# A split-precision encoder layer on one core: another order for the first token tiles of the value projection

## What is computed

```python
proj = x @ w_in
qa, ka, va, qb, kb, vb = jnp.split(proj, cuts, axis=-1)   # va: 128 columns, vb: 512
...
oa, _ = banded_attention(qa, ka, va, ...)     # windowed, with sinks and ALiBi
ob = dilated_attention(qb, kb, vb, ...)       # three dilations, merged
return jnp.concatenate([rms_norm(oa, norm_a), rms_norm(ob, norm_b)], -1) @ w_out
```

## Time and profile before

| | us |
|---|---|
| runs, median (lowest to highest) | 1284.3 (1279.02 to 1286.18) |
| the profiled execution | 1276.83 |
| its span, first to last instruction | 1275.0 |
| TensorE busy | 1212.4 (95%) |
| VectorE busy | 734.3 (58%) |
| ScalarE busy | 579.1 (45%) |
| GpSimd busy | 213.5 (17%) |
| mean granted TensorE clock | 0.977 |

### The profile page before, as it was taken

One profiled execution on the slowest core, in us unless ns is written; L12 is line 12 of the kernel. 1 busy time (PEld: TensorE's weight loads), 2 busy tenths in 40 slices (PEclk: granted clock), 3 DMA queues, 4 the chain that ended last, 5 costly groups with the idle time before them and its releaser, 6 DMA issues.

```text
span 1275.0 us, 22105 instructions
## 1 busy us (share of the span) xinstructions
PE 1212.4 (95%) x8045; PEld 1089.4 (85%) x8045; DVE 734.3 (58%) x1790; ACT 579.1 (45%) x1416; POOL 213.5 (17%) x276
## 2 busy tenths in 40 slices
PE   7999999999999999998899999998899999999993
PEld 6998788888888888887687888897799999999892
DVE  3232355665665556554667887548666556665478
ACT  3332244543554444434443343220366666666455
POOL 0120001200120021001111122000223323333222
PEclk9999999999999999999899999999899999999997
DMA  7697664365437453678535333442799999999783
GB/s 231 223 300 247 157 152 102 76 172 115 113 83 183 96 123 89 157 192 229 163 120 189 127 136 117 157 169 67 239 307 276 289 287 272 272 280 302 190 306 145
DMA packets 165106, 237.47 MB, mean 186 GB/s; under 512 B 41584, under 2 KB 111472, under 8 KB 164976
## 3 DMA queue, kind: packets, MB, share of 16 engines
q1 hardware_dynamic: 146096, 176.61, 46.0%
q0 software_dynamic: 11776, 41.95, 13.3%
q10 hardware_dynamic: 7152, 17.83, 4.3%
HBM read 147.44 MB, written 59.02 MB: 162 GB/s over the span
## 4 chain that ended last, share of the span: by engine, by line
PE 79%; issue 6%; DVE 4%; DMA 4%; SPq 2%; ACT 2%; POOL 1%; DVEq 1%; ACTq 0%; POOLq 0%
PE bank L843 18%; PE bank L845 17%; PE bank L844 17%; PE bank L944 9%; PE bank L837 5%; PE bank L931 5%; PE bank L922 4%; PE bank L923 2%; SPq L583 2%; PE bank L1066 2%; DMA Q<-stage_lo 1%; DMA KA<-stage_lo 1%; SPq L579 1%; DMA a_work<-in_x 1%; DMA d_work<-x_scratch,idc 1%
## 5 line engine op out<-in xcount | busy, mean ns | idle before, releaser
L1330 ACT ACTIVATE b_work<-b_work 128x256 f32<-128x256 f32 (+3 forms) x288 | 148.0, 514 | 244.9 <-DVE b_work L1680 244.8
L843 PE MATMUL bank<-xgT_hi,w_gu_hi 128*128 128x224 f32 (+1 forms) x704 | 197.6, 281 | 4.4 <-ACT d_work L1562 2.3
L844 PE MATMUL bank<-xgT_lo,w_gu_hi 128*128 128x224 f32 (+1 forms) x704 | 196.4, 279 | 0.0
L845 PE MATMUL bank<-xgT_hi,w_gu_lo 128*128 128x224 f32 (+1 forms) x704 | 196.3, 279 | 0.0
L1689 DVE COPY b_work<-bank 128x256 f32<-128x256 f32 (+2 forms) x256 | 112.7, 440 | 125.4 <-PE bank L931 124.6
L843 PEld LDWEIGHTS bank<-xgT_hi,w_gu_hi 128*128 128x128 f32 x704 | 136.7, 194 | 6.6 <-issue 3.1
L844 PEld LDWEIGHTS bank<-xgT_lo,w_gu_hi 128*128 128x128 f32 x704 | 136.7, 194 | 0.7
L845 PEld LDWEIGHTS bank<-xgT_hi,w_gu_lo 128*128 128x128 f32 x704 | 136.9, 194 | 0.0
L2196 POOL CAST Q<-Q 128x512 fp32r<-128x512 f32 x48 | 52.1, 1117 | 451.0 <-DVE w_k_lo L1636 236.5
L931 PE MATMUL bank<-keep,b_work 128*128 128x128 f32 x608 | 115.2, 275 | 6.2 <-ACT b_work L1330 6.2
L931 PEld LDWEIGHTS bank<-keep,b_work 128*128 128x128 f32 x608 | 80.5, 140 | 41.3 <-ACT b_work L1330 11.5
(11 more groups left out here) (214 smaller groups left out, 2844.8 us busy)
## 6 DMA issues: line engine op xcount, KB each, us to landing
raw_gu<-in_w_gate SPq DMA_DIRECT2D x32, 512.0 KB, 8.7
raw_gu<-in_w_up SPq DMA_DIRECT2D x32, 512.0 KB, 9.5
raw_d<-in_w_down SPq DMA_DIRECT2D x16, 1024.0 KB, 9.6
Q<-stage_hi SPq DMA_DIRECT2D x96, 128.0 KB, 2.4
Q<-stage_lo SPq DMA_DIRECT2D x96, 128.0 KB, 2.4
o_scratch<-b_work SPq DMA_DIRECT2D x36, 264.0 KB, 3.3
c_work<-o_scratch SPq DMA_DIRECT2D x12, 792.0 KB, 5.6
wo_scratch<-a_work POOLq DMA_DIRECT2D x16, 512.0 KB, 5.5
```

The lines of the kernel that those rows point to most:

```text
L843: nc.tensor.matmul(o, w_hi, x_hi, start=first, stop=False)
L844: nc.tensor.matmul(o, w_hi, x_lo, start=False, stop=False)
L845: return nc.tensor.matmul(o, w_lo, x_hi, start=False, stop=last)
L1330: nc.scalar.activation(prob[:, u % 2, 0:n], prob[:, u % 2, 0:n], ACT.Exp, scale=-1.0, bias=o[:, HD:HD + 1], accum_out=o[:, HD + 1:HD + 2])\
```

## The change

Seven edits, all in the first stage:

1. TensorE's queue begins with six 128x128 products of a tile of ones, into bank 7, which nothing reads. They wait only for VectorE's memset of the ones.
2. SyncE issues the identity ahead of x 0, and x 1 behind the first value slab's two loads.
3. For tiles 0 and 1 the hand-over of `xT` goes by halves of four pieces (one bank): new semaphores `xt_half`, `xs_half`, `xts_half`. Tile 1's banks are 2 and 3 as before. ScalarE and VectorE take half a tile and a weight slab by turns.
4. TensorE's loop over slabs starts a tile when its first half is there and asks for the second half at slab 4.
5. Tile 2 is transposed behind slab 5 of that loop, not after it. TensorE's wait for `v_ready` of tile 0, which ScalarE's order implied before, is now written out ahead of tile 2's products.
6. x 4 is no longer behind the first store of values, the three loads of gains stand ahead of it, and the other small loads behind x 5.
7. The eight steps of the output weights are each one tile earlier.

```diff
-WO_TILES = (3, 4, 5, 6, 7, 8, 9, 10)
+WO_TILES = (2, 3, 4, 5, 6, 7, 8, 9)
...
+            sp.dma_start(ident, const[:, 0:P]).then_inc(S["id_loaded"], 16)
             sp.dma_start(xin[:, 0, :], x_t[0]).then_inc(x_ld[0], 16)
-            sp.dma_start(ident, const[:, 0:P]).then_inc(S["id_loaded"], 16)
-            sp.dma_start(xin[:, 1, :], x_t[1]).then_inc(x_ld[1], 16)
             for k in range(KD):
+                if k == 1:
+                    sp.dma_start(xin[:, 1, :], x_t[1]).then_inc(x_ld[1], 16)
...
             load_w(KA0, KA0 + HD)
+            load_gains()
+            load_x(4)
             for t in range(4, TILES):
                 store_v(t - 4)
-                load_x(t)
-                if t == 4:
+                if t > 4:
+                    load_x(t)
+                if t == 5:
                     load_small()
...
+            pe.wait_ge(S["ones_ready"], 1)
+            for c in range(6):
+                nc.tensor.matmul(bank[7][:, 0:P], ones, ones, start=True, stop=True)
             pe.wait_ge(S["id_loaded"], 16)
+
+            def xt_first(t):
+                pe.wait_ge(x_ld[t], 16)
+                for c in range(KD):
+                    made = nc.tensor.transpose(bank[2 * t + c // 4][:, P * (c % 4):P * (c % 4) + P],
+                                               xin[:, t, P * c:P * c + P], ident)
+                    if c % 4 == 3:
+                        made.then_inc(S["xt_made" if c > 4 else "xt_half"], 1)
...
                 pe.wait_ge(S["xts_ready"], t + 1)
+                if t == 2:
+                    pe.wait_ge(S["v_ready"], 1)
...
-            xt(0)
-            xt(1)
-            pe.wait_ge(S["xts_ready"], 2)
+            xt_first(0)
+            xt_first(1)
             for k in range(KD):
                 pe.wait_ge(S["wv_made"], k + 1)
                 for t in range(2):
+                    if k == 0:
+                        pe.wait_ge(S["xts_half"], t + 1)
+                    if k == KD // 2:
+                        pe.wait_ge(S["xts_ready"], t + 1)
                     for c in range(2):
                         last = vpart(t, k, c)
                     if k == KD - 1:
                         last.then_inc(S["v_made"], 1)
-            xt(2)
+                if k == 5:
+                    xt(2)
...
-            xt(0)
-            xt(1)
-            for k in range(KD):
+            def xt_part(t, c):
+
+                act.wait_ge(S["xt_made" if c else "xt_half"], t + 1)
+                copy(xT[:, 0, 0, 4 * c:4 * c + 4, P * t:P * t + P],
+                     bank[2 * t + c][:].rearrange("p (k c) -> p k c", c=P)).then_inc(S["xs_hi" if c else "xs_half"], 1)
+
+            def wv_high(k):
+
                 act.wait_ge(S[f"wv_ld{k}"], 32)
                 copy(wv_hi[:, 640 * k:640 * k + 640], raw_v[:, k, :]).then_inc(S["wv_hi"], 1)
+
+            xt_part(0, 0)
+            wv_high(0)
+            xt_part(0, 1)
+            xt_part(1, 0)
+            wv_high(1)
+            xt_part(1, 1)
+            for k in range(2, KD):
+                wv_high(k)
+            xt(2)
             for t in range(TILES):
-                if 1 <= t < TILES - 1:
+                if 2 <= t < TILES - 1:
                     xt(t + 1)
```

More of the change, by code:

```diff
@@ L360, in encoder_layer @@
         bank = [ctx.enter_context(nc.psum_tensor(f"bank{b}", [P, 512], FP32)) for b in range(8)]
-        names = """id_loaded c_loaded x_ld0 x_ld1 xt_made xts_ready
+        names = """ones_ready id_loaded c_loaded x_ld0 x_ld1 xt_half xs_half xts_half xt_made xts_ready
             v_made v_ready vb_st0 vb_st1 proj_made proj_hi proj_ready dup_done dup_q ta_loaded t1_loaded t2_loaded
@@ L592, in load_small, with load_gains @@
                                  allow_slow_non_contiguous=True).then_inc(S["wr_loaded"], 16)
+            def load_gains():
                 for c in range(2):
@@ L1613, in _ @@
             V = nc.vector
-            V.memset(ones, 1.0)
+            V.memset(ones, 1.0).then_inc(S["ones_ready"], 1)
             V.memset(eps_ln, LN_EPS)
@@ L1643, in proj_low, with xt_part, wv_low @@
                 V.tensor_tensor(lo, sums, plain(hi), ALU.subtract).then_inc(S["proj_ready"], 1)
-            xt(0)
-            xt(1)
-            for k in range(KD):
+            def xt_part(t, c):
+                dve.wait_ge(S["xs_hi" if c else "xs_half"], t + 1)
+                hi, lo = (xT[:, 0, part, 4 * c:4 * c + 4, P * t:P * t + P] for part in range(2))
+                V.tensor_tensor(lo, bank[2 * t + c][:].rearrange("p (k c) -> p k c", c=P), plain(hi), ALU.subtract)\
+                 .then_inc(S["xts_ready" if c else "xts_half"], 1)
+            def wv_low(k):
                 dve.wait_ge(S["wv_hi"], k + 1)
@@ L1650, in _ @@
                                 plain(wv_hi[:, 640 * k:640 * k + 640]), ALU.subtract).then_inc(S["wv_made"], 1)
+            xt_part(0, 0)
+            wv_low(0)
+            xt_part(0, 1)
+            xt_part(1, 0)
+            wv_low(1)
+            xt_part(1, 1)
+            for k in range(2, KD):
+                wv_low(k)
             def wo_low(k):
```

## The result

The changed kernel is slower. In 14 runs of each its median is 1287.68 us (1286.12 to 1294.02) and that of the kernel before 1283.19 (1278.79 to 1286.18); the measured ratio is 1.005, with a 95% interval of 1.0035 to 1.0066 (the quotient of the two medians alone is 1.0035). The forecast was 1278 with a range of 1271 to 1284, so the time lies outside it, on the slow side. "Slower by over 0.5%" had a chance of 0.04, and the ratio stands just at that bound.

What follows compares the result with a forecast made beforehand. TensorE, busy 95% of the 1275.0 us span, was taken as the bound. Gains 2.9 (start) + 0.9 (clock) + 1.7 (tile 2) + 0.6 (x 5) = 6.1 us gave 1278 us on the runs' median of 1284.3, range 1271 to 1284.

Steps and rivals of the forecast that it cites:

- the one on the output weights: Output weights one tile earlier: same splits, loads and stores, load chain keeps its place relative to its tile; counted as 0.
- The slack of 1.4 us at tile 11: Tightest place for the output weights: VectorE finishes tile 11's x at 100.5, TensorE starts it at 101.9.
- Rival 4: Output weights' chain falls behind, in-order ScalarE makes tiles 6 to 11 late; TensorE loses 9.6 us, 1287.8 us; chance 0.04.
- Start: Up to tile 2's first value matmul, forecast near 24.7 instead of 30.42: 5.5 us earlier, bounds 4.7 to 6.3.
- the term of 2.9: Value matmuls of tiles 0 and 1 begin earlier through half-tile hand-over and the new load order: 2.7 to 3.1 us.
- rival 3: Reordering fails: x 1 lands at 9 us or later, TensorE idles as long as before; 2.8 us gained, 1281.5; chance 0.06.
- Clock: First value matmuls run at full clock sooner because TensorE works from 1.1 us: 0 to 1.4 us, taken as 0.9.
- The price of the ones: Six products of ones at the head of TensorE's queue end by 3.5 us, at most 4.3, before x 0: no cost.
- Tile 2 inside the loop: Tile 2 transposed behind slab 5, its copies made under slabs 6 and 7, removes TensorE's wait: 1.7 us.
- x 4 and x 5: x 5 issued ahead of the small loads saves TensorE's wait, 0.6 us; x 4 behind the early loads costs nothing.
- the wait on `v_ready`: New TensorE wait ahead of tile 2's matmuls: costs nothing; 0.9 us were both covers gone.
- The norm_a loads: Put ahead of x 4 in SyncE's queue, they cost nothing: 1.72 us, at most 2.3, on a cover of 7.

Runs made afterwards that it cites:

- e1: Changed kernel with the output weights' eight steps put back behind tiles 3 to 10; ratio 0.9978 to the kernel before.
- e3: Kernel before with only the output weights moved one tile earlier, behind tiles 2 to 9; ratio 1.0019 to the kernel before.
- f4: f3 with x 1 issued third again, ahead of all weight slabs; ratio 0.9961 to the kernel before.
- f3: f1 with all small loads also moved ahead of x 4; ratio 0.9973 to the kernel before.
- f1: Changed kernel with ScalarE and VectorE doing the next tile's x copies ahead of the output weights; ratio 1.0016 to the kernel before.
- f2: Changed kernel with GpSimd issuing each output-weight store ahead of the wait for the store before it; ratio 1.0127 to the kernel before.
- e4: Changed kernel with x 4 on and the small loads in the old order and output weights back behind tiles 3 to 10; ratio 1.0011 to the kernel before.
- g3: f4 without the six products of ones; ratio 0.9935 to the kernel before, 1272.11 us against 1281.11.
- g4: f4 with the output weights back behind tiles 3 to 10; ratio 0.9993 to the kernel before.

## Why the prediction was wrong

**The step that failed** is the one on the output weights: "I count 0 here, as the load chain keeps its place relative to its tile". It does keep its place relative to its tile, but not relative to the quiet stretch of the DMA engines, which stands at nearly the same time in both kernels: the earlier start and the earlier tile together shifted the first store from behind it into it. The term counted as 0 measured 8.7 us of the stage (117.6 against e1's 108.9). The sentence beside it, "an earlier start moves bytes to where there is room", drew on a DMA share of 0.40 at 20 to 30 us; what counted was 34 to 39 us, for which the prediction read no stretch. The kernel before has, there:

```profile
34.00:35.00 1.00, 1.00 (x8) 1.00 (x8) 0.00 (x0) 0.00 (x0) 0.00 (x0) 1.00 0.05 0
35.00:39.00 4.00, 4.00 (x35) 4.00 (x34) 0.00 (x0) 1.20 (x4) 0.00 (x0) 1.00 0.05 0
```

That row, with the first store 12 us earlier, was the warning. The slack of 1.4 us at tile 11 was read rightly, and the first hold alone, 12.2 for 5.3 us, is beyond it. The earlier place also costs without the hold, 4.9 us in e3, and the prediction had no term for that either.

**Rival 4** described what happened, place and mechanism: ScalarE in order, tiles 6 to 11 late. It had 6 tiles x 1.6 us = 9.6; the trace has six waits with 9.0 and a further 2.5 us of clock, and a start that gave less. That its 1287.8 us is so near the 1287.68 measured is in part luck: it is 3.5 above the median of 1284.3, and the ratio makes 6.4. Its evidence against, "the same bytes start one tile earlier", was the error above turned round.

**Start, forecast 2.9 + 0.9 + 1.7 = 5.5 us by tile 2; measured 4.3,** and over the nine kernels with this head 3.1 in the median (2.5 to 4.7). Tile 2 gave its 1.6 and the clock 0.8 (below), so that 1.9 are left for the term of 2.9. The identity was there at 2.7, 2.0 us behind its issue; x 0 took 4.0 us instead of 3.6 and the first transpose came at 5.28, not 4.7. But the miss is x 1. Behind slab 0's loads it took 5.5 us from issue to landing, not the 4.4 of the earlier trace rows, and TensorE waited 1.74 us for it. That is rival 3 in part. f4 shows it from the other side: issued third, tile 2 starts 0.8 us earlier than here, and 2.6 earlier than in f3, which differs in nothing else.

**Clock, forecast 0.9 us of 1.4: 0.8 here, by luck.** From 9.70 to 11.0 the products went at the lower level, which lost (1 − 0.18/0.32) x 1.3 = 0.6 where 1.4 was lost before. Of the nine kernels with this head only the changed one, f1 and f2 have it so; in the other six the lower level lasted to between 13.0 and 14.1 us, nearly as long as before, though the products began 1.0 to 1.9 us earlier, so that this term gave nothing (e4: 9.92 to 14.0, 1.8 lost). And the way there was another. In the profiled execution the eight first transposes ran at the full clock (1.06 us), and TensorE fell back to 0.50 while it waited for x 1:

```profile
5.00:6.00 1.00, 0.72 (x7) 0.75 (x8) 0.00 (x0) 0.06 (x1) 0.00 (x0) 1.00 1.04 228
...
7.00:8.00 1.00, 0.00 (x0) 0.00 (x0) 1.00 (x3) 0.65 (x2) 0.00 (x0) 0.72 1.02 346
8.00:10.00 2.00, 1.92 (x9) 1.92 (x10) 0.76 (x3) 0.76 (x2) 0.00 (x0) 0.50 1.06 381
```

Full level was reached that early in 3 of the 11 profiles with ones (after, f1, f3); in the other eight the first eight transposes took 1.94 us or the sixteen 3.65. The forecast's reason against a fall, gaps "much shorter than that 3.3", didn't hold: the clock fell in 1.74 us of idle here. Nor does the length of a gap decide it alone: behind e3's wait of 1.86 us it fell, behind f1's of 2.98 us near 100 us it stayed at 1.00. Where the sixteen transposes run without a gap between them (g3, f4, g4), the value products are at the full level by 9.0 to 10.4 us, and in g3, which has no ones, first of all (0.18 apart from 8.99 on). The rule of the Trainium skill that the prediction cites ("TensorE: Matmul & The Clock Gate", "What's actually happening"), that activity releases the throttle, agrees with the three profiles; the other eight don't show the ones doing it. By it all 1.4 us would have come, and 0.8 did. The price of the ones was right in that they are over at 3.96, before x 0. But the five records of the earlier trace rows are not five products: as with `x12` above, each fp32 product there stands as two records, so that the 0.10 us was the spacing of halves.

**Tile 2 inside the loop, x 4 and x 5, the wait on `v_ready`: right.** No wait stands at any of them. The norm_a loads took 4.6 us of SyncE's queue, more than the bound of 2.3, on a cover of 7. The term of 0.6 for x 5 was too small by what e4 showed: the load order was worth 3.2 us of the stage.

**The account of the stage.** Forecast 6.1 earlier, measured 7.7 later, 13.8 apart: 9.0 us of waits for `xT`, 2.5 of clock behind them, 1.2 at the start; 1.1 us stays open. In e1, without edit 7, the same account closes: 5.1 us behind the forecast's 103.8, 2.3 of them at the start (tile 2 at 27.21) and 2.8 in one wait for `xT`.

**The chances.** 0.04 for rival 4 was too little. Its deciding point was a wait 2.4 us longer a tile; ScalarE's wait for output weights grew by 30.7 us over six tiles, 5.1 each, in a chain that waits for every store.

## What to carry to other kernels

A chain of load, compute, store that waits for each store has its own period; before it is moved, read from the trace what the DMA engines do in the very microseconds into which its first transfer will fall, not the mean around them. On an engine that executes in order, put the work that the bottleneck waits for ahead of the work whose data comes late, as f1 did, and a slow chain costs less than half (3.7 us for 9.0). And price a start that is made earlier together with the next load that it will run into: e4 won 2.8 us and lost them 15 us later.

## What the runs showed of the hardware that was not expected

- Two loads that spread single fp32 values over all partitions, 2 KB each, were 8.1 to 11.4 us on their way, and for about 5 us of that the 16 DMA engines moved about 1 GB/s in the mean, 597 packets under 512 B, with stores and loads of both queues pending. It followed these loads wherever they were issued: at 18, 20 and 31 us (for 2 us only where they were issued at 18). What stops the rest isn't shown.
- A granted clock of 1.00 at the head of a profile is no evidence: with that record eight transposes took 1.06 us in some executions and 1.94 in others.
- A 128x128 fp32 product of ones takes 0.49 us of TensorE at the lower clock (2.93 us for six; their weight loads take 0.333 us each, against 0.192 at the full clock). It stands as two records in the profile. The estimates of 0.40 and 0.54 were both worked out from records taken for products, so that the nearness of 0.54 is chance.
- Nine executions with the same head begin tile 2's products over a range of 2.2 us, 25.75 to 27.95. One profile of each kernel can't rank starts that lie closer than that.
